# Thirty products of constants taken out of seven normalisations of a two-block transformer kernel

## The reference, cut to what matters

```python
def first_block(x, ...):
    h = layer_norm(x, ln0_g, ln0_b)
    for l in range(DEPTH):
        proj = h @ w_in[l]
        ...
        h = layer_norm(ALPHA * h + mix, ln1_g[l], ln1_b[l])
        f = conv_glu_ffn(h, w_up[l], w_fconv[l], b_fconv[l], w_down[l])
        h = layer_norm(ALPHA * h + f, ln2_g[l], ln2_b[l])
    return h

def second_block(x, c, ...):
    c_act = jax.nn.silu(c)
    for l in range(DEPTH):
        mod = c_act @ w_ada[l] + b_ada[l]
        sh1, sc1, g1, sh2, sc2, g2 = jnp.split(mod, 6, axis=-1)
        h = modulate(rmsnorm(x, norm_mix_g[l]), sh1, sc1)
        ...
        x = x + g1[:, None, :] * y
        h = modulate(rmsnorm(x, norm_ffn_g[l]), sh2, sc2)
        f = swiglu(...) if l % 2 == 0 else moe_swiglu(...)
        x = x + g2[:, None, :] * f
    return x
```

## Time and profile before

| | before |
|---|---|
| median of three runs | 2059.1 us (2058.98 to 2060.08) |
| profiled execution | 2059.45 us, span 2057.5 us |
| PE busy | 2032.9 us, 99% |
| DVE busy | 1746.6 us, 85% |
| ACT busy | 1348.8 us, 66% |
| the chain that ended last | 90% on PE |

### The profile page before, as it was taken

How to read it: one execution, slowest core, us unless ns; L and a number is a source line. 1 busy time by engine, 2 the same in 40 slices (tenths; PEclk the granted TensorE clock), 3 DMA queues, 4 the chain that set the end, 5 groups by cost and what they waited for, 6 DMA issues and landing times.

```text
span 2057.5 us, 31713 instructions
## 1 busy us (share of the span) xinstructions
PE 2032.9 (99%) x12976; PEld 1799.3 (87%) x12976; DVE 1746.6 (85%) x2237; ACT 1348.8 (66%) x1874; POOL 3.6 (0%) x23
## 2 busy tenths in 40 slices
PE   9999999999999999999999999999999999999998
PEld 8899999899998799999778888888888888888886
DVE  6788886789887867787879998998989989899997
ACT  5665545665545574445667777777777777777775
POOL 0000000000000000000000000000000000000000
PEclk9999999999999999999999999999999999999999
DMA  5358783358784538785449999999999999899994
GB/s 201 127 214 281 256 297 133 133 200 289 250 297 178 173 143 297 251 297 209 146 175 361 368 364 352 353 364 371 360 362 346 370 369 362 350 348 370 368 364 187
DMA packets 94038, 578.05 MB, mean 281 GB/s; under 512 B 11584, under 2 KB 14656, under 8 KB 35648
## 3 DMA queue, kind: packets, MB, share of 16 engines
q1 hardware_dynamic: 92592, 570.03, 74.8%
q0 software_dynamic: 288, 3.15, 0.4%
q10 hardware_dynamic: 1008, 2.80, 0.4%
HBM read 571.75 MB, written 1.05 MB: 278 GB/s over the span
## 4 chain that ended last, share of the span: by engine, by line
PE 90%; DVE 5%; ACT 2%; DMA 1%; issue 1%; SPq 0%; DVEq 0%; ACTq 0%
PE bank L2178 46%; PE bank L523 43%; PE bank L2237 1%; DVE wlo L1463 1%; DMA side<-in_w_ada 1%; DMA ring<-in_w_in 0%; DMA xT<-in_xT 0%; DVE side L1599 0%; ACT whi L1077 0%; PE bank L963 0%; ACT arena L1216 0%; DVE xT L2377 0%; DVE XC L1520 0%; DVE arena L1732 0%; DVE arena L1675 0%
## 5 line engine op out<-in xcount | busy, mean ns | idle before, releaser
L1463 DVE TENSOR_TENSOR wlo_moe<-ring,whi_moe 128x1024 fp32r<-128x1024 f32 x448 | 525.0, 1217 | 6.6 <-ACT whi_moe L1077 4.7
L1077 ACT ACTIVATE whi_moe<-ring 128x1024 fp32r<-128x1024 f32 x448 | 460.2, 1060 | 61.2 <-PE bank L2178 57.0
L523 PE MATMUL bank<-HH,whi 128*128 128x256 f32 x1536 | 430.7, 280 | 0.8 <-DVE wlo L1463 0.8
L523 PE MATMUL bank<-HL,whi 128*128 128x256 f32 x1536 | 424.4, 276 | 0.0
L523 PE MATMUL bank<-HH,wlo 128*128 128x256 f32 x1536 | 424.4, 276 | 0.0
L1463 DVE TENSOR_TENSOR wlo<-ring,whi 128x1024 fp32r<-128x1024 f32 (+3 forms) x318 | 343.5, 1112 | 73.4 <-ACT whi L1077 73.2
L1077 ACT ACTIVATE whi<-ring 128x1024 fp32r<-128x1024 f32 (+3 forms) x318 | 297.3, 966 | 93.9 <-PE bank L523 78.5
L523 PEld LDWEIGHTS bank<-HH,whi 128*128 128x128 f32 x1536 | 288.3, 188 | 4.0 <-DVE wlo L1463 1.8
L523 PEld LDWEIGHTS bank<-HL,whi 128*128 128x128 f32 x1536 | 288.4, 188 | 1.0 <-issue 0.5
L523 PEld LDWEIGHTS bank<-HH,wlo 128*128 128x128 f32 x1536 | 288.4, 188 | 0.0
L1463 DVE TENSOR_TENSOR extra_lo<-ring,extra_hi 128x1024 fp32r<-128x1024 f32 x224 | 264.1, 1219 | 14.4 <-ACT extra_hi L1077 14.1
(11 more groups left out here) (305 smaller groups left out, 3586.0 us busy)
## 6 DMA issues: line engine op xcount, KB each, us to landing
ring<-in_moe_gate SPq DMA_DIRECT2D x112, 1024.0 KB, 6.3
ring<-in_moe_up SPq DMA_DIRECT2D x112, 1024.0 KB, 7.0
ring<-in_moe_down SPq DMA_DIRECT2D x112, 1024.0 KB, 6.4
side<-in_w_ada SPq DMA_DIRECT2D x96, 512.0 KB, 4.3
ring<-in_w_up SPq DMA_DIRECT2D x44, 1024.0 KB, 4.9
ring<-in_w_in SPq DMA_DIRECT2D x32, 1024.0 KB, 5.3
ring<-in_w_down SPq DMA_DIRECT2D x32, 704.0 KB, 4.5
ring<-in_ffn_gu SPq DMA_DIRECT2D x22, 1024.0 KB, 5.5
```

Of the source, the lines that this page charges most:

```text
L523: return pe.matmul(out, lhsT, rhs, start=start, stop=stop, skip_group_check=True)
L1077: a.activation(hi, part, ACT.Copy).then_inc(*made.up(("hi", n, i)))
L1463: v.tensor_tensor(lo, part, hi.bitcast(F32), ALU.subtract).then_inc(*done.up(("lo", n, i)))
```

## The change

`busy` is not called at the end of a normalisation in `HALVED`. The modulation's sums stay in their places, and so do the constants behind `ln2` of layer 1 and `rms1` of layer 1, those ahead of `ln0`, and those behind the router's counts.

```diff
                 for g in sums:
                     mod_sums(g)
-                if end:
+                if end and s.name not in HALVED:
                     busy(end, s.name)
```

## The result

The changed kernel takes 2068.45 us (median of six runs, 2066.65 to 2072.9) against 2059.26 (six runs, 2058.98 to 2060.5): 9.2 us more, a ratio of 1.0042, 95% interval 1.0031 to 1.0053. I had forecast 2060.0 and a range up to 2067.5.

A forecast was written before the change was run, and what follows sets the result against it. TensorE, busy 99% of the span, was taken to bound the kernel. From 2059.1 us, a direct gain of 0.6 and one clock fall of 1.5 gave +0.9, so 2060.0; the 8-in-10 range was 2057.5 to 2067.5.

The forecast's parts named there:

- What bounds it, and the two levels: Whole program: TensorE busy 99% of the span, chain on PE for 90%; clock levels 2.4 and 1.2 GHz.
- What the change removes: Seven normalisations: thirty unread products of constants, 60 rows of 0.23 us, given as 13 us of TensorE's busy time.
- The direct gain: Earlier products on `hT`, chiefly 0.90 us at `rms0` of layer 1, 0.3 lost to DVE: 0.6 taken, bounds 0 and 0.94.
- The price of one fall: Raw pair behind a silence: one drop of TensorE's clock costs 1.5 us, with bounds 0 and 7.3.
- The number of falls: Clock falls in the one or two longest silences, `ln0` and perhaps `ln1` of layer 0; chance 0.38.
- What it may cost: Seven places: silences up to 3.83 us may drop the clock; interpolated chances 0.87, 0.54 and 0.22, then lowered.
- the upper end of the forecast: Two falls, at `ln0` and `ln1` of layer 0: +2.4 us; forecast times 2060.0 to 2061.5.
- the second rival: Clock falls in three or more places, those with modulation's sums among them: +3.9 to +9.9 us; chance 0.28.
- The banks: Everywhere: seven `take` calls go, so products use a bank one earlier in the round of eight; priced at nothing.
- What would show it: Clock slices dip at 17, perhaps 133 us; `ln0` rows take 8.8 us; lower clock around 325, 440 or 643: second rival.
- The signs of being wrong altogether: A fall lasting much longer than 3 us, or a stretch away from the seven places changing by more than 1 us.

The follow-up runs named there:

- all_2: The changed kernel once more, on one chip with its two parts, against the kernel before: 2070.00 us, ratio 1.0050.
- f_ln0: The kernel before with the constants left out at `ln0` alone: 2063.09 us, ratio 1.0011.
- a_bank: The changed kernel, except that the seven normalisations still take their banks, with no product of constants issued into them: 2069.46 us, ratio 1.0041 against before.
- e_late: The kernel before with eleven constants in place of six at `ln1` of layer 0, nothing left out: 2061.56 us, ratio 1.0005.
- l_held: The kernel before with 64-column sums at five places, more constants at three idle places and fewer at `rms0` of layer 1: 2059.56 us, ratio 0.9998.

## Why the prediction was wrong, point by point

**What bounds it, and the two levels.** Right: the chain stayed on PE, and the falls of TensorE's clock are the largest part of the loss. The Trainium skill's page "TensorE: Matmul & The Clock Gate", section "Why this matters for your kernels", warns of idle gaps in mid-kernel. The trace agrees now at `ln0` and `ln1` of layer 0, 0.50 behind 3.82 and 3.14 us of silence; idle time alone does not account for the falls behind 1.45 and 0.77 us, nor for the clock that held behind 2.45.

**What the change removes.** 60 rows of 0.23 us are 13.8 us, not 13. TensorE's busy time fell by 2.4 us only.

**The direct gain.** Right. At `rms0` of layer 1 the products on `hT` start 0.78 us behind the sums (948.37 + 1.84 = 950.21 to 950.99) where it was 1.68. At the other places the first tile of `hT` releases them, as predicted. That 0.3 of the gain is lost to DVE shows in `all_2`, where this place held: against the trace of before, the pair behind the raw one has come 0.83 us nearer, and the next, which needs the first `wlo` half, keeps 0.5 of that.

**The price of one fall.** Right: 1.5 us was taken, `f_ln0` gives 1.6, and the falls of 3.4 us in the changed kernel 1.5 to 1.7. Some falls last twice as long.

**The number of falls.** Here it failed, at the step "What it may cost". `ln0` and `ln1` of layer 0 fell, as the upper end of the forecast had it; `ln2`, `ln1` of layer 1 and `rms0` of layer 1 fell too. I measured each place by its silence, from the last row of any kind to the next, and set the chance of a fall by where that length lies between one silence that held and one that did not. So I gave the four places with the modulation's sums, 1.46 us and less of silence, no share in the sum, and left them to the second rival at 0.28. They fell 16 times of 21. The one-column rows did not cover: where the same rows had 64 columns, one place of eight fell, in two traces. The argument that I set against the rival, that 1.7 us of such rows left the clock up in the kernel before, was read from rows with constants behind them, the cover that the change takes away. The three silent places fell 15 times of 19, where my lowered chances stood for about one of three. And the silence of 1.99 us that stood for "held" was one draw: thirteen traces have it, at 2.0 us, and in seven of them the clock fell right behind it, at 638.

**The second rival** was the result. It named the places, and at five falls its sum is -0.6 + 5 x 1.5 = 6.9, where the raw pairs and the gain give 7.8. My range ended at its sixth fall, 2067.5, and 2068.45 was measured: I gave no room to long falls, and none to the 1.5 us that came away from the seven places.

**The banks.** Right: nothing, by `a_bank`.

**What would show it.** The slices of the clock could not show it, as a fall is a fifteenth of a slice. The clock's column read less at 329, 445 and 951 us, which was named as the sign of the second rival; the raw pair at `ln0` took 9.55 us where 8.8 was named for one fall. The signs of being wrong altogether both came: the low stretch at `ln0` lasted 6.8 us, and the stretch from 457 to 634 us grew by 1.8.

**Left open.** Why a place falls in one run and not in the next, and whether the falls at 638 (seven of the fourteen traces) and 1070 (five) come more often when something is left out. The traces of before, `e_late`, `l_held` and both traces of the whole change have neither, `a_bank` has the one at 638, so a rule was not found. The spread of before itself (2058.34 to 2064.43) goes in part with the clock: of its 60 runs in the three sets, the nine with a mean granted clock of 1.000 took 2058.96 to 2059.92 us and the four with 0.997 took 2063.65 to 2064.43, against 0.992 to 0.994 in the six runs of the change. Which places fell in them is not known; the one profile has no fall before the last product. DVE's waits for the modulation's weights grew from 2.5 to 5.8 us in the profile of the change, but were 2.8 in that of `a_bank` with the same loss. So they are not the cause of the whole, though one of them cost 1.2 us at 619 us; whether the change makes them more likely is not shown.

## What to carry to other kernels

Products that nobody reads can be worth their place: ask of each what TensorE would do instead, and look at the clock in stretches of a few us behind it, not in the slices of the page. When cover is judged, count what is multiplied in a stretch and not how many rows stand in it: one-column products kept TensorE busy in the profile, and its clock fell behind them in 16 places of 21. An effect that changes from run to run needs several traces per kernel; one trace of before, without a fall, said little about how near each place was, and the silence that it showed as harmless was not.

## What the runs showed of the hardware that I had not expected

The granted clock fell behind 0.77 us of silence (with sixteen one-column rows of 1.84 us ahead of it) and held behind 2.45 us in the same trace. Sixteen sums of 64 columns took 1.89 us where those of one column took 1.84, with the next row 1.40 us behind them for 1.45, and the clock held in seven places of eight. It fell also at two places that keep their constants in every kernel, at 638 (behind 2.0 us of silence) in seven traces of fourteen and at 1070 in five.
